# Key sums one level earlier, K turned one level later, the bonus product behind W: a reordering of the RWKV-7 chunk stage

## The chip, the cores and the metric

One core of a Trainium2 chip. The metric is the device time of one execution in microseconds (us). The kernel is written out instruction by instruction for five engines that run side by side: TensorE (PE, with its weight loads as PEld), VectorE (DVE), ScalarE (ACT), GpSimd (POOL) and SyncE (SP, which here only issues DMAs). Each engine takes its instructions strictly in the order in which they are written; engines meet only at semaphores.

## The reference, cut to what matters

One layer of a hybrid backbone over 2048 latent and 256 context tokens: norm, one wide input projection, four mixers in parallel, gates, an output projection. The change touches only one of the mixers, a two-way RWKV-7 recurrence over 4 heads of 64:

```
kk = to_heads(k * lp['rw_kk'])
kk = kk / jnp.maximum(jnp.sqrt(jnp.sum(kk * kk, axis=-1, keepdims=True)), 1e-12)
for d in range(2):
    w = -jax.nn.softplus(-(lp['rw_w0'][d] + jnp.tanh(w_lo) @ lp['rw_w2'][d])) - 0.5
    decay = to_heads(jnp.exp(-jnp.exp(w)))
    a = to_heads(jax.nn.sigmoid(lp['rw_a0'][d] + a_lo @ lp['rw_a2'][d]))
    kd = kh * (1.0 + (a - 1.0) * k_a)
    y, s_fin = wkv7_scan(rh, decay, kd, vh, -kk, kk * a, s0[d], reverse=(d == 1))
    bonus.append(jnp.sum(rh * kd * r_k, axis=-1, keepdims=True) * vh)
# one step of the scan
sa = jnp.einsum('bhvk,bhk->bhv', S, a_t)
S = S * w_t[:, :, None, :] + sa[..., :, None] * b_t[..., None, :] + v_t[..., :, None] * k_t[..., None, :]
```

The kernel computes the scan in chunks of 64 tokens. In each chunk the operands are scaled by the running decay ("hats": A from kk, R from r, K from kd, B from kk * a), a 64x64 triangular matrix is inverted by doubling, and what comes out are a map of the state (P), an addition to it (Q) and two terms of the output.

## The kernel before

`recurrence_local_stage` (from 1310 to 1788 us of the trace) works on 9 blocks of 256 tokens, each in two directions: 18 passes, d = 0 and d = 1 in turn, called `unit` on each engine. While a pass runs, the next one is prepared between its steps, so 17 passes hold a preparation: the 9 of d = 0 prepare d = 1 of the same block, 8 of d = 1 prepare d = 0 of the next block. That second preparation is the longer one: it also mixes the token rows and computes the inverse norm of kk.

TensorE's order in a pass, for the levels v = 1 to 5 of the inversion (`unit` in the tensor block): the product Gv (rows of the trace `rw_ps<-inv,m_b`), something beside it (`beside`), then Xv (`rw_ps<-inv_g,inv_t`) and Zv (`rw_ps<-inv_t,inv_g`), then something between (`between`). VectorE must mask Gv before Xv can start (`inv_g<-rw_ps`); ScalarE copies Xv and Zv to SBUF (`inv`, `inv_t`) before the next level's products can read them. At level 5 there is no X5.

- Beside level 3 stand a product of the preparation (`a_lora`, `rw_ps<-z_mixed,lora`) and the turning of K hat for the current pass (`rw_ps<-ident,k_hat`), which ScalarE copies out as `k_rows`. Between 3 and 4: `rw_ps<-head_centre,z_mixed` (V).
- Beside level 4 stand the key sums (`rw_ps<-heads,kk_sq`, in bank 4, where X4 is written too, so X4 waits until VectorE has read them into `kk_norm_sq`, "nx"). In a d = 1 pass VectorE then takes ten short dependent steps of Newton's method (`norms`, n0 to n2c) and spreads the result into rows (`kk_norm_rows`, "rx"). In a d = 0 pass the key sums are computed too, but nobody reads them.
- Between 4 and 5: `rw_ps<-ident,a_r_hat` (A). ScalarE copies it out as `w_in_rows` ("At."), and a second copy to the other half of that tile follows ("MV.").
- Beside level 5: `rw_ps<-v_rows,m_k`, and then the turning of the norm rows (`norm_columns`, `rw_ps<-ident,kk_norm_rows`, "rnT"), which is written to bank 7 and so waits for the copy At. Then Z5.
- Then the bonus product (`rw_ps<-kd_sum,heads`), W (`rw_ps<-w_in_rows,inv_t`), which waits for ScalarE's copy of Z5, and the first product of the next pass (`first_scores`, `rw_ps<-a_r_hat,b_hat`), which waits for VectorE's last hat; then GY (`rw_ps<-m_r,w_rows` and `rw_ps<-m_k,v_rows`).

ScalarE holds, besides the copies, the preparation's activations: `k_rate` (key rates, `key_rates`), and `exps`: `e_padded` (EI), `e_neg` (EN) and a tiny copy `chunk_decay` (tot). VectorE holds the scan of the logs (`decay`, `log_run`), `norms`, `rates` (`k_d`) and, at the end of the pass, `hats`.

Semaphores count results in a fixed order per engine (class `Turns`); the lists at the head of the stage (`prep_v`, `main_a`, `main_p` and others) name that order, and `after(engine, unit, result)` waits for one.

## Time and profile before

| | us |
|---|---|
| median of 3 runs | 2466.56 |
| lowest and highest | 2465.54, 2466.60 |
| the profiled execution's own time | 2462.29 |
| its span, first to last instruction | 2460.6 |
| TensorE busy, whole span | 2263.6 (92%) |
| VectorE busy | 1551.8 (63%) |
| ScalarE busy | 1009.5 (41%) |
| mean granted TensorE clock | 0.969 |

Busy time is what the profiler recorded for instructions of an engine; a matmul's end is modelled. A row of the timeline gives the start in us from the span's start, the duration, engine, line, operation, and what is written from what; in square brackets stands how long the engine was idle just before it and which instruction ended that. An f32 matmul is recorded as two, so 16 matmuls read x32. Neighbouring groups overlap in the rows by about 0.2 us because matmuls are pipelined; the distance from start to start is what a group costs.

### The profile page before, as it was taken

Reading aid. Unit: us, or ns where it says so; the run is one execution under the profiler, and the core shown is the slowest. Engines: PE = TensorE matmul, PEld = TensorE weight load, DVE = VectorE, ACT = ScalarE, POOL = GpSimd, SP = SyncE. Lnnn points to the kernel's source line nnn. Section 1 sums busy time; section 2 is a strip of 40 time slices with the busy share of each in tenths; the row PEclk is TensorE's granted clock in tenths of the full one; section 3 lists DMA queues with packets and bytes.
Section 4 is the critical chain, followed back from the end, with each engine's and each line's share of the span. In section 5 each row is a group of like instructions: output and inputs, shape, how many; then the busy total and the mean of one; then the engine's idle time right before and its main releaser. Section 6 shows DMA issues by size and latency. Waiting matters only on the chain. (4 is left out here: it accounts for less than half of the span.)

```text
span 2460.6 us, 66375 instructions
## 1 busy us (share of the span) xinstructions
PE 2263.6 (92%) x26630; PEld 1853.4 (75%) x26630; DVE 1551.8 (63%) x2611; ACT 1009.5 (41%) x1734; POOL 265.3 (11%) x335
## 2 busy tenths in 40 slices
PE   4999999999899999999947899999788799899998
PEld 2788878888688887888836777777657576688887
DVE  5756566666865456665635777777456676856754
ACT  5444234544532123445424555555333666411111
POOL 0000000000000000000031222222124663000000
PEclk7999999999999999999978999999978899999999
DMA  7344333333242333333330111110068523834542
GB/s 240 107 135 125 111 94 111 113 117 102 94 129 93 96 108 97 106 111 119 107 101 25 32 41 32 32 56 17 19 214 305 126 94 95 288 115 171 197 152 88
DMA packets 250306, 277.75 MB, mean 113 GB/s; under 512 B 30683, under 2 KB 174171, under 8 KB 247643
## 3 DMA queue, kind: packets, MB, share of 16 engines
q1 hardware_dynamic: 245306, 266.95, 33.9%
q10 hardware_dynamic: 4576, 8.40, 0.9%
q8 instruction: 70, 1.15, 0.2%
q0 software_dynamic: 320, 0.98, 0.2%
q14 instruction: 34, 0.27, 0.0%
HBM read 184.66 MB, written 91.62 MB: 112 GB/s over the span
## 5 line engine op out<-in xcount | busy, mean ns | idle before, releaser
L715 PE MATMUL proj_ps<-h_hi,w_hi 128*128 128x512 f32 x1656 | 649.5, 392 | 27.6 <-DVE h_lo L465 19.7
L716 PE MATMUL proj_ps<-h_lo,w_hi 128*128 128x512 f32 x1656 | 647.0, 391 | 0.0
L717 PE MATMUL proj_ps<-h_hi,w_lo 128*128 128x512 f32 x1656 | 646.4, 390 | 0.0
L318 ACT CAST w_hi<-w_raw 128x512 fp32r<-128x512 f32 x420 | 255.1, 621 | 694.0 <-PE proj_ps L717 353.2
L715 PEld LDWEIGHTS proj_ps<-h_hi,w_hi 128*128 128x128 f32 x1656 | 312.3, 189 | 98.2 <-issue 26.1
L717 PEld LDWEIGHTS proj_ps<-h_hi,w_lo 128*128 128x128 f32 x1656 | 312.2, 189 | 65.6
L716 PEld LDWEIGHTS proj_ps<-h_lo,w_hi 128*128 128x128 f32 x1656 | 312.4, 189 | 62.9
L482 DVE TENSOR_TENSOR w_lo<-w_raw,w_hi 128x512 fp32r<-128x512 f32 x420 | 283.2, 689 | 44.3 <-ACT w_hi L318 43.7
L498 DVE TENSOR_TENSOR z_slots<-proj_ps,x_rows 128x512 f32<-128x512 f32 x174 | 120.2, 691 | 169.9 <-PE proj_ps L717 167.9
L498 DVE TENSOR_TENSOR x_rows<-proj_ps,x_rows 128x512 f32<-128x512 f32 x116 | 80.1, 691 | 108.9 <-PE proj_ps L717 102.9
L1010 POOL MEMSET rpb_padded<- 60x127 f32 x1 | 0.2, 198 | 1261.3 <-POOLq L89 1261.3
L1211 DVE TENSOR_TENSOR inv_g<-rw_ps,level_masks 128x512 f32<-128x512 f32 x90 | 62.1, 690 | 97.2 <-PE rw_ps L1387 97.1
L2903 PE MATMUL late_ps<-late_lo,mw_hi 128*128 128x512 f32 x252 | 98.0, 389 | 0.0
L1334 ACT COPY inv<-rw_ps 128x512 f32<-128x512 f32 x72 | 42.0, 583 | 125.0 <-PE rw_ps L1387 125.0
L494 DVE COPY x_rows<-proj_ps 128x512 f32<-128x512 f32 x58 | 40.0, 690 | 73.6 <-PE proj_ps L717 73.5
L2492 DVE CUSTOM_DVE_ANT_0 scores<-na_ps,bias_windows 128x768 f32<-128x768 f32 x64 | 61.3, 957 | 34.4 <-issue 25.3
L2448 ACT ACTIVATE late_rows<-scores,softmax_stats 128x768 f32<-128x768 f32 x64 | 60.1, 940 | 52.3 <-DVE softmax_stats L2495 52.3
L2945 PE MATMUL late_ps<-wo_hi,y_hi 128*128 128x512 f32 x208 | 81.3, 391 | 0.0
L2947 PE MATMUL late_ps<-wo_hi,y_lo 128*128 128x512 f32 x208 | 81.0, 389 | 0.0
L2946 PE MATMUL late_ps<-wo_lo,y_hi 128*128 128x512 f32 x208 | 80.9, 389 | 0.0
L332 ACT ACTIVATE z_slots<-z_slots 128x512 f32<-128x512 f32 x128 | 70.6, 621 | 14.1 <-DVE z_slots L498 9.0
L2728 ACT ACTIVATE late_ps<-late_rows 128x1024 f32<-128x1024 f32 x15 | 15.4, 1030 | 125.8 <-DVE late_rows L2818 125.8
(380 smaller groups left out, 4101.4 us busy)
## 6 DMA issues: line engine op xcount, KB each, us to landing
w_raw<-in_w_in SPq DMA_DIRECT2D x240, 256.0 KB, 3.0
scratch_gatesT<-z_slots SPq DMA_DIRECT2D x128, 256.0 KB, 2.7
late_rows<-scratch_gatesT SPq DMA_DIRECT2D x64, 512.0 KB, 4.4
scratch_zT<-z_slots SPq DMA_DIRECT2D x108, 256.0 KB, 2.4
ada<-in_ada_w SPq DMA_DIRECT2D x4, 2048.0 KB, 15.2
late_rows<-scratch_zT SPq DMA_DIRECT2D x4, 2048.0 KB, 12.7
late_rows<-scratch_branchT SPq DMA_DIRECT2D x16, 512.0 KB, 5.3
late_rows<-in_x SPq DMA_DIRECT2D x16, 512.0 KB, 4.9
```

The costliest lines, as they stand in the source:

```text
L318: A.copy(wh[:, i, :, :], raw[:, q, :, :]).then_inc(w_hi, 1)
L332: A.activation(zs[:, q, :], zs[:, q, :], ACT.Sigmoid).then_inc(gated, 1)
L482: V.tensor_tensor(wl[:, i, :, :], raw[:, W_SOURCE[i], :, :], wh[:, i, :, :].bitcast(F32), ALU.subtract).then_inc(w_lo, 1)
L498: V.tensor_tensor(to, ps[:, BANK[n], :], part[:, {1: 0, 3: 0, 4: 2, 5: 0, 6: 1}[n], :], ALU.add).then_inc(ev, 1)
L715: T.matmul(out, wh[:, i, k, :], hi[:, o, k, :], start=(first and k == 0), stop=False, skip_group_check=not first)
L716: T.matmul(out, wh[:, i, k, :], lo[:, o, k, :], start=False, stop=False, skip_group_check=not first)
L717: last = T.matmul(out, wl[:, i, k, :], hi[:, o, k, :], start=False, stop=(k == 3), skip_group_check=not first)
L1211: done(V.tensor_tensor(eights(G[:]), ps[:, 2:4, 0:256].rearrange("p q (k t) -> p q k t", t=CH), mask, ALU.mult), f"G{v}.", *(("P0.", "Q0." ...
L2903: T.matmul(o, hi, b_lo[:, i % 2, k, :], start=False, stop=False)
L2945: T.matmul(o, y_hi[:, k, rows], wo_hi[:, k, cols], start=(k == 0), stop=False)
L2946: T.matmul(o, y_hi[:, k, rows], wo_lo[:, k, cols], start=False, stop=False)
L2947: last = T.matmul(o, y_lo[:, k, rows], wo_hi[:, k, cols], start=False, stop=(k == KT - 1))
```

## The change

It moves instructions of the stage; the arithmetic is the same. On TensorE the key sums go from beside level 4 to beside level 3, where they take the place of K's turning, which goes beside level 4; the wait for nx goes from X4 to X3, and the bonus product goes behind W. On ScalarE the key rates stay behind the third Z but now come ahead of the copy V; EI goes ahead of the copy of K's rows, and EN and tot go ahead of the copy At. On VectorE nx goes ahead of the scan and the ten Newton steps behind it, both to level 3; the spreading (rx) stays at level 4; one hat (R, or kk * a for d = 1) moves to an earlier place, and the last hat is now K, not B.

```
@@ beside(v), tensor block
                     if v == 3:
                         if more:
                             a_lora(u, -1)
+                            key_sums(u, -1)
+                    if v == 4:
                         main_a.after(pe, u, "Bt.")
                         go()
                         turned(Kh, "K.")
-                    if v == 4 and more:
-                        key_sums(u, -1)
@@ between(v)
                     if v == 4:
-                        main_a.after(pe, u, "V.")
+                        main_a.after(pe, u, "Kt.")
@@ unit, tensor block
-                    if v == 4 and more:
+                    if v == 3 and more:
                         prep_v.after(pe, u, "nx", -1)
...
-                if more:
-                    prep_v.after(pe, u, "bt", -1)
-                    go()
-                    prep_p.done(mm(ps[:, 6, :], J[:], flat(kds[:])), 0, "bonus")
                 main_a.after(pe, u, "Z5.")
...
                 done(last, "W.")
                 if more:
+                    prep_v.after(pe, u, "bt", -1)
+                    go()
+                    prep_p.done(mm(ps[:, 6, :], J[:], flat(kds[:])), 0, "bonus")
                     first_scores(u, -1)
@@ first_scores, tensor block
-                prep_v.after(pe, u, "B", back)
+                prep_v.after(pe, u, "K", back)
@@ unit, scalar block
                 factor(X[:], "X3.", 4)
                 factor(Z[:], "Z3.", 0)
-                rows(Kt, "Kt.", "K.")
+                if nxt:
+                    key_rates(*nxt)
                 if d == 0:
                     main_p.after(act, (n, d), "V.")
                     own(A.copy(flat(Vt[:]), ps[:, 6, :]), "V.")
                 if nxt:
-                    key_rates(*nxt)
+                    exp_up(*nxt)
+                rows(Kt, "Kt.", "K.")
                 factor(X[:], "X4.", 4)
                 factor(Z[:], "Z4.", 0)
+                if nxt:
+                    exp_down(*nxt)
                 main_p.after(act, (n, d), "A.")
                 own(A.copy(eights(WI[:, :, :, :, 0:CH]), ps[:, 6:8, 0:256].rearrange("p q (k t) -> p q k t", t=CH)), "At.")
-                if nxt:
-                    exps(*nxt)
@@ unit, vector block
                     if v == 3 and nxt:
+                        if d:
+                            norm_squares(nxt[0])
                         decay(*nxt)
+                        if d:
+                            norms(nxt[0])
+                        else:
+                            key_rate_hat(*nxt)
                     if v == 4 and nxt:
                         if d:
-                            norms(nxt[0])
+                            norm_rows(nxt[0])
                         rates(*nxt)
                         if d == 0:
                             bonus_rows(n)
+                        else:
+                            query_hat(*nxt)
@@ new helpers (exp_up is the first half of exps, exp_down its rest: EN and tot)
+            def norm_squares(n):
+                prep_p.after(dve, (n, 0), "ks")
+                prep_v.done(V.tensor_scalar(nx[:], ps[:, 4, 0:8], 1e-24, None, ALU.max), 0, "nx")
+            def key_rate_hat(n, d):
+                prep_a.after(dve, (n, d), "ta1")
+                prep_v.done(V.scalar_tensor_tensor(kka[:], aa[:], 1.0, kk[:], ALU.add, ALU.mult), d, f"kka{d}")
+            def query_hat(n, d):
+                prep_a.after(dve, (n, d), "EI")
+                if not (first_block(n) and d == 0):
+                    main_g.after(dve, (n, d), "R.", back=1)
+                prep_v.done(V.tensor_tensor(chunks(AR[:, 1, :, :]), chunks(zf[:, 0:2, :]), padded(d, 1 - d), ALU.mult), d, "R")
@@ hats: what is left, in the new order
+                if d:
+                    query_hat(n, d)
+                else:
                     prep_p.after(dve, (n, 0), "rnT")
                     done(V.tensor_tensor(kk[:], kkr[:], ps[:, 7, :].rearrange("p (m t) -> p m t", m=2), ALU.mult), "kk")
+                    prep_v.after(dve, (n, 0), "kk")
+                    key_rate_hat(n, d)
...
                 done(V.scalar_tensor_tensor(chunks(AR[:, 0, :, :]), chunks(kk[:]), -1.0, padded(d, d), ALU.mult, ALU.mult), "A")
+                prep_v.after(dve, (n, d), f"kka{d}")
+                prep_a.after(dve, (n, d), "EN")
+                done(V.scalar_tensor_tensor(Bh[:], kka[:], 0.5, EN[:], ALU.mult, ALU.mult), "B")
                 prep_v.after(dve, (n, d), "kd")
                 done(V.tensor_tensor(Kh[:], kd[:, d], EN[:], ALU.mult), "K")
-                prep_v.after(dve, (n, d), "kka")
-                done(V.scalar_tensor_tensor(Bh[:], kka[:], 0.5, EN[:], ALU.mult, ALU.mult), "B")
```

The result lists of the semaphores follow the new order; the preparation ahead of the first pass takes its steps in the new order too.

TensorE's queue in a pass, from the second preparation product beside level 3 to X3, before (`main_` and `prep_` semaphores belong to the current pass and to the preparation):

```order
L1387 MATMUL rw_ps<-z_mixed,lora 128x256 [waits prep_scalar]
L1387 MATMUL rw_ps<-z_mixed,lora 128x256
L1448 MATMUL rw_ps<-ident,k_hat 128x128 [waits main_scalar]
L1448 MATMUL rw_ps<-ident,k_hat 128x128 x3
L858 REGISTER_ALU
L1387 MATMUL rw_ps<-inv_g,inv_t 64x64 [waits main_scalar,main_vector]
```

and now (the line numbers are those of the changed kernel):

```order
L1416 MATMUL rw_ps<-z_mixed,lora 128x256 [waits prep_scalar]
L1416 MATMUL rw_ps<-z_mixed,lora 128x256
L1416 MATMUL rw_ps<-heads,kk_sq 128x2 [waits prep_vector]
L1416 MATMUL rw_ps<-heads,kk_sq 128x2 x3
L858 REGISTER_ALU
L858 REGISTER_ALU [waits main_scalar]
L1416 MATMUL rw_ps<-inv_g,inv_t 64x64 [waits prep_vector,main_vector]
```

K's turning has left this place, the key sums stand in it, and X3 behind them waits for `prep_vector` (nx) as well.

ScalarE's queue in a d = 1 pass from the third Z to the copies into `w_in_rows`, before:

```order
L1334 COPY inv_t<-rw_ps 128x512 [waits main_products]
L1338 COPY k_rows<-rw_ps 128x512 [waits main_products]
L1305 ACTIVATE k_rate<-a_tanh,one_less_half_ka,half_ka 128x256 [waits prep_scalar]
L1305 ACTIVATE k_rate<-a_tanh,one_less_half_ka,half_ka 128x256
L1334 COPY inv<-rw_ps 128x512 [waits main_products]
L1334 COPY inv_t<-rw_ps 128x512 [waits main_products]
L1367 COPY w_in_rows<-rw_ps 128x8x64 [waits main_products]
L1311 ACTIVATE e_padded<-log_run 128x8x64 [waits prep_vector]
L1312 ACTIVATE e_neg<-log_run 128x512
L1315 COPY chunk_decay<-e_padded 128x8 [waits prep_scalar]
L1371 COPY w_in_rows<-rw_ps 128x8x64 [waits main_products]
```

and now:

```order
L1361 COPY inv_t<-rw_ps 128x512 [waits main_products]
L1330 ACTIVATE k_rate<-a_tanh,one_less_half_ka,half_ka 128x256 [waits prep_scalar]
L1330 ACTIVATE k_rate<-a_tanh,one_less_half_ka,half_ka 128x256
L1334 ACTIVATE e_padded<-log_run 128x8x64 [waits prep_vector]
L1365 COPY k_rows<-rw_ps 128x512 [waits main_products]
L1361 COPY inv<-rw_ps 128x512 [waits main_products]
L1361 COPY inv_t<-rw_ps 128x512 [waits main_products]
L1338 ACTIVATE e_neg<-log_run 128x512
L1341 COPY chunk_decay<-e_padded 128x8 [waits prep_scalar]
L1398 COPY w_in_rows<-rw_ps 128x8x64 [waits main_products]
L1400 COPY w_in_rows<-rw_ps 128x8x64 [waits main_products]
```

Two instructions, `e_neg` and `chunk_decay`, now stand between the copy of Z4 and the first copy into `w_in_rows`; before, they stood behind it.

## Rows read from the trace of the kernel before

**Rows 1.** Busy time by stretch; columns as in the first row.
```profile
core 0: us, PE busy (x) PEld busy (x) DVE busy (x) ACT busy (x) POOL busy (x), PEclk, DMA share, GB/s
...
1310.00:1788.00 478.00, 422.83 (x15574) 362.83 (x15574) 327.54 (x633) 256.70 (x546) 103.49 (x95) 1.00 0.11 33
```

**Rows 2.** TensorE's waits, 1310 to 1788: us in total, times, longest.
```profile
PE rw_ps L1387 <- DVE b_hat L1152: 14.0, 17, 0.9
...
PE rw_ps L1387 <- DVE kk_norm_inv L1120: 3.5, 8, 0.4
```

**Rows 3.** TensorE timeline, d = 1 pass: start, us, ..., [idle before].
```profile
1505.75 0.66 PE L1448 MATMUL rw_ps<-ident,k_hat 128*128 128x128 f32 x4
1506.33 0.69 PE L1387 MATMUL rw_ps<-inv_g,inv_t 64*64 64x64 f32 x32
...
1508.51 0.69 PE L1387 MATMUL rw_ps<-inv,m_b 64*64 64x64 f32 x32
1509.14 1.05 PE L1387 MATMUL rw_ps<-heads,kk_sq 128*128 128x2 f32 x8
1510.63 0.69 PE L1387 MATMUL rw_ps<-inv_g,inv_t 64*64 64x64 f32 x32 [0.44 <-DVE kk_norm_inv L1120]
...
1513.21 0.66 PE L1426 MATMUL rw_ps<-ident,kk_norm_rows 128*128 128x128 f32 x4
1514.17 0.69 PE L1387 MATMUL rw_ps<-inv_t,inv_g 64*64 64x64 f32 x32 [0.30 <-issue]
1514.80 1.12 PE L1387 MATMUL rw_ps<-kd_sum,heads 128*128 128x512 f32 x2
1515.85 1.10 PE L1387 MATMUL rw_ps<-w_in_rows,inv_t 64*64 64x128 f32 x32
1517.82 1.10 PE L1387 MATMUL rw_ps<-a_r_hat,b_hat 64*64 64x128 f32 x32 [0.86 <-DVE b_hat L1152]
1518.71 0.44 PE L1387 MATMUL rw_ps<-m_r,w_rows 64*64 64x64 f32 x16
```

**Rows 4.** ScalarE timeline, the same pass.
```profile
1512.34 0.61 ACT L1367 COPY w_in_rows<-rw_ps 128x512 f32<-128x512 f32 x1
...
1513.35 0.65 ACT L1312 ACTIVATE e_neg<-log_run 128x512 f32<-128x512 f32 x1
...
1513.97 0.61 ACT L1371 COPY w_in_rows<-rw_ps 128x512 f32<-128x512 f32 x1
1514.92 0.59 ACT L1334 COPY inv_t<-rw_ps 128x512 f32<-128x512 f32 x1 [0.35 <-PE rw_ps L1387]
```

**Rows 5.** VectorE timeline, the same pass.
```profile
1505.94 1.22 DVE L1109 TENSOR_TENSOR_SCAN log_run<-scan_keep,log_w 128x512 f32<-128x512 f32 x1
1509.28 0.69 DVE L1211 TENSOR_TENSOR inv_g<-rw_ps,level_masks 128x512 f32<-128x512 f32 x1 [2.11 <-PE rw_ps L1387]
1510.23 0.17 DVE L1119 TENSOR_SCALAR kk_norm_sq<-rw_ps 128x8 f32<-128x8 f32 x1 [0.26 <-PE rw_ps L1387]
...
1512.44 0.43 DVE L1125 COPY kk_norm_rows<-kk_norm_inv 128x512 f32<-128x512 f32 x1
```

**Rows 6.** TensorE timeline, d = 0 pass.
```profile
1534.68 0.69 PE L1387 MATMUL rw_ps<-inv,m_b 64*64 64x64 f32 x32
1535.31 1.05 PE L1387 MATMUL rw_ps<-heads,kk_sq 128*128 128x2 f32 x8
1536.29 0.69 PE L1387 MATMUL rw_ps<-inv_g,inv_t 64*64 64x64 f32 x32
...
1539.46 0.69 PE L1387 MATMUL rw_ps<-inv_t,inv_g 64*64 64x64 f32 x32
...
1543.12 1.10 PE L1387 MATMUL rw_ps<-a_r_hat,b_hat 64*64 64x128 f32 x32 [0.87 <-DVE b_hat L1152]
```

**Rows 7.** VectorE timeline before the first pass.
```profile
1293.99 1.22 DVE L1109 TENSOR_TENSOR_SCAN log_run<-scan_keep,log_w 128x512 f32<-128x512 f32 x1
1297.51 0.17 DVE L1119 TENSOR_SCALAR kk_norm_sq<-rw_ps 128x8 f32<-128x8 f32 x1 [2.30 <-PE rw_ps L1387]
```

More of the change, by code:

```diff
@@ L918, in recurrence_local_stage @@
         U = 64
-        mixes, newton = [f"{j}" for j in (6, 2, 3, 0, 1, 4, 5)], ["nx", "n0"] + [f"n{i}{x}" for i in range(3) for x in "abc"] + ["rx"]
-        block_v = [f"mix{j}" for j in mixes] + ["ksq"] + newton + ["kk"]
+        mixes, newton = [f"{j}" for j in (6, 2, 3, 0, 1, 4, 5)], ["n0"] + [f"n{i}{x}" for i in range(3) for x in "abc"]
+        block_v = [f"mix{j}" for j in mixes] + ["ksq", "nx"] + newton + ["rx", "kk"]
         block_a = [f"scaled{j}" for j in mixes] + ["th", "kkr0", "kkr1", "rrk0", "rrk1"]
-        prep_v = Turns(ctx, nc, "prep_vector", [f"mix{j}" for j in mixes] + ["ksq", "lw", "L", "Lx", "inc"] + newton
-                       + ["kd", "kds", "bt", "kk", "R", "kka", "A", "K", "B", "bonus"], U,
-                       leaves_out=(("Lx", "inc", "kds", "bt", "bonus"), block_v))
+        prep_v = Turns(ctx, nc, "prep_vector", [f"mix{j}" for j in mixes] + ["ksq", "nx", "lw", "L", "Lx", "inc"] + newton + ["kka1", "rx", "kd"]
+                       + ["kds", "bt", "R", "kk", "kka0", "A", "B", "K", "bonus"], U,
+                       leaves_out=(("Lx", "inc", "kka1", "kds", "bt", "bonus"), block_v + ["kka0"]))
         prep_a = Turns(ctx, nc, "prep_scalar", [f"scaled{j}" for j in mixes]
@@ L1117, in norms @@
                 i32 = mybir.dt.int32
-                prep_p.after(dve, (n, 0), "ks")
-                own(V.tensor_scalar(nx[:], ps[:, 4, 0:8], 1e-24, None, ALU.max), "nx")
                 own(V.tensor_scalar(ny[:].bitcast(i32), nx[:].bitcast(i32), -0.5, 1597463007.0, ALU.mult, ALU.add), "n0")
@@ L1179, in prologue @@
                 key_squares(0)
+                norm_squares(0)
                 decay(0, 0)
                 norms(0)
+                norm_rows(0)
                 rates(0, 0)
+                query_hat(0, 0)
                 hats(0, 0)
@@ L1305, in key_rates, with exp_up, exp_down @@
                     prep_a.done(A.activation(uu[:, m, :], aa[:, m, :], ACT.Identity, scale=hka[:, m:m + 1], bias=oka[:, m:m + 1]), d, f"u{m}")
-            def exps(n, d):
+            def exp_up(n, d):
+                prep_v.after(act, (n, d), "inc" if d else "L")
+                prep_a.done(A.activation(padded(d, 1 - d), chunks((inc if d else L)[:]), ACT.Exp, scale=0.5 * DECAY), d, "EI")
+            def exp_down(n, d):
                 own = lambda ins, name: prep_a.done(ins, d, name)
-                prep_v.after(act, (n, d), "inc" if d else "L")
-                run = chunks((inc if d else L)[:])
-                own(A.activation(padded(d, 1 - d), run, ACT.Exp, scale=0.5 * DECAY), "EI")
                 own(A.activation(EN[:], (inc if d else L)[:], ACT.Exp, scale=-0.5 * DECAY), "EN")
@@ L1325, in prologue @@
                 key_rates(0, 0)
-                exps(0, 0)
+                exp_up(0, 0)
+                exp_down(0, 0)
                 act.sem_inc(main_a.sem, main_a.each)
```

15 lines of the change are left out of this document (5 added, 10 removed).

## Prediction

> **What bounds the kernel now.** I read the busy time by stretch first, then TensorE's waits in the stage that the change touches, then the timelines of three engines over two neighbouring passes. In the stage from 1310 to 1788 us TensorE is busy 422.8 of 478 us at the full granted clock, 1.00 [rows 1]: it is the bound, and time can only come from its waits or from work that it would no longer do. The change takes no work from it. The waits are few and regular: 14.0 us for VectorE's last hat ahead of the next pass's first product, 17 times, and 3.5 us, 8 times, ahead of X4 in d = 1 passes, where the view names the instruction behind nx [rows 2]. The question is how far each product starts later or earlier than before, and I follow that through one d = 1 and one d = 0 pass. Everything after the next pass's first product hangs on it by the same waits as before, so a shift there is the shift of the whole pass.
>
> **d = 1 pass (8 times).** Key sums at level 3. They start where K's turning stood, at 1505.75. Where they stand now, nx starts 1.09 us after them (1509.14 to 1510.23) and X4, waiting for it, 1.49 after them (1509.14 to 1510.63) [rows 3, 5]. X3 therefore starts at 1505.75 + 1.49 = 1507.24 and not at 1506.33: +0.91. G4, behind it, comes at about 1509.40.
>
> The Newton steps ahead of G4's mask. VectorE now waits with the scan until nx is read: nx at 1506.84, then the short op on log_w and the scan, which starts about 0.6 later and takes 1.22 [rows 5], so it ends near 1508.7. The ten steps follow; from nx to rx were 2.21 us, 0.20 of it nx itself, so they last 2.0 and end at 1510.7 [rows 5]. The mask of G4 stands behind them. It started 0.77 after G4 (1508.51 to 1509.28) [rows 3, 5] and would be wanted at 1510.17, so it is 0.5 late. In the d = 0 pass X4 starts 1.61 after G4 (1534.68 to 1536.29) [rows 6]: 0.77 to the mask, 0.69 for it, 0.15 to X4. So X4 follows the mask's start by 0.85 and comes at 1511.55 against 1510.63: +0.92. K's turning, now beside G4, takes 0.58 (1505.75 to 1506.33) and lies under this. Bounds: if the Newton steps were free, X4 would be 1.61 after G4, as in the d = 0 pass [rows 6], and the shift +0.4; if each small op cost some more for the wait between them, +1.1. I take 0.92, from the rows of the same ops.
>
> EN and tot ahead of the copy At. EN starts at 1513.35 and the copy behind tot at 1513.97, so the pair costs ScalarE 0.62 [rows 4]. At follows X4 by 1.71 (1510.63 to 1512.34), now by 2.33. Is anyone waiting? The norm rows' turning starts at 1513.21; At ended at 1512.34 + 0.61 = 1512.95, 0.26 before [rows 3, 4]. The product ahead of it is only 16 short matmuls, so I read the turning as waiting for At, and the 0.62 goes through in full. If it were TensorE's own queue that held it, up to 0.6 less: this is the lower bound. The turning takes 0.58, so Z5 starts at 1511.55 + 2.33 + 0.87 + 0.58 = 1515.33 against 1514.17: +1.16. (The old Z5 stood 0.96 after the turning, since G5's mask was late; that wait goes.)
>
> The bonus behind W. ScalarE's copy of Z5 starts at 1514.92 and takes 0.59; 0.15 later W can start, that is 1.49 after Z5. Before, the bonus product (1514.80 to 1515.85, 1.05) held W until 1.68 after Z5: 0.2 gained there [rows 3, 4]. W gives way to the next group after some 0.9, as the equal-shaped first product does (1517.82 to 1518.71). So W at 1516.82, bonus at 1517.71, first product at 1518.76 at the earliest. VectorE: the turned norms end at 1514.75 + 0.66 = 1515.41; then kk, kk * a (0.12 more, as it waits for kk), A, B, K at 0.60 each, and 0.68 + 0.15 to the first product: 1518.80. Both against 1517.82: +1.0. The old idle 0.86 ahead of the first product is gone, but the bonus fills it and the pass is not shorter.
>
> **d = 0 pass (9 times).** Nobody waits for nx here, so only the key sums' length against K's counts: 1.05 busy with a last matmul of 0.25, so about 0.93 from start to start, at most 0.98 (1535.31 to 1536.29) [rows 6], less 0.58: +0.35 at X3. At level 4 X4 is 1.61 after G4 because of the mask, and K's turning fits under that: +0.35. EN and tot: +0.62. Z5 is at +0.97. From Z5 to the first product are now 1.49 + 0.9 + 1.05 = 3.44 against 3.66 (1539.46 to 1543.12) [rows 6]: +0.75. The hat kk * a of d = 1 lies in VectorE's idle time ahead of G4, and the last hat is ready before TensorE asks.
>
> **Ahead of the first pass.** The scan ended before nx (1293.99 + 1.22 against 1297.51) and now stands behind it [rows 7]; some 1.8 us of it and the log come ahead of the Newton steps, of which one hat fewer behind rnT and a stall behind the Newton steps give back most. I take +0.5, between 0.3 and 1.2. The last pass has no preparation: no change.
>
> **A rule against one of these terms.** The row: eight passes of the key sums, with only 2 columns each, take 1.05 us [rows 3]. The Trainium skill, "TensorE: Matmul & The Clock Gate", section "Back-to-back issue gap", gives for 1 to 64 columns an issue floor of about 25 ns; by that the key sums would be some 0.2 us, shorter than K's turning, and X3 in a d = 0 pass would come 0.4 earlier and not 0.35 later. The same page's section "LDWEIGHTS" lets a load of 128 columns take 107 ns, which is near what the row shows. By the first rule the nine d = 0 passes alone would be 9 x 0.7 = 6.3 us cheaper and the sum some 9 us instead of 15. The measured row decides, and it speaks for the longer figure.
>
> **Sum.** 8 x 1.0 + 9 x 0.75 + 0.5 = 8.0 + 6.75 + 0.5 = 15.3 us. The profiled execution took 2462.29 us and would take 2477.6. It lies 4.27 below the median of 2466.56; by the median the forecast is 2481.8, rounded 2482.
>
> **Rivals.**
> 1. ScalarE's EN and tot are covered: the norm rows' turning did not wait for At. For it: the product ahead of it starts only some 0.6 before. Against: the steady 0.26 behind At's end. Then the d = 0 pass shifts by 0.13 and the d = 1 pass by 0.4: 8 x 0.4 + 9 x 0.13 + 0.5 = 4.9, 2471.5 us, on the edge of no change. 10%.
> 2. Faster: TensorE's waits on VectorE are the whole price. The mechanism is at the end of the pass and at X3: key sums cost there no more than K's turning did, nx is ready before X3 is due, and the earlier hats let the bonus run in the idle time before the first product. It decides if nx comes within 0.6 us of the key sums' start and EN is covered. Then a d = 0 pass gains the 0.2 at W, a d = 1 pass that, the 0.44 ahead of X4 and the 0.38 of the late G5 mask: 9 x 0.2 + 8 x 1.0 = 10, 2456.6 us. For it are the 17.5 us of waits in [rows 2]; against it the 1.09 us that nx took. 6%.
> 3. Much slower: TensorE's clock. It is 1.00 in the stage with idle times below 0.9 us [rows 1, 3]. The new wait ahead of X3 is 0.44 us, and ahead of X4 it is 0.8 or so. Should these waits bring it to its lower level (1.2 instead of 2.4 GHz), products take twice as long there; for 2 us of products in each d = 1 pass that is 8 x 2 = 16 on top, 2498 us. The rows show no fall in 478 us after idle times nearly as long. The Trainium skill, "TensorE: Matmul & The Clock Gate", section "Part 1: The HAM clock gate", says that activity releases the throttle and idleness brings it back. That the clock stayed at 1.00 through the waits of before does not contradict it. This rival has 4%.
>
> **Numbers.** The forecast's own case has 80%. Within it the terms are uncertain by 0.4 us per pass at most, mostly downwards (Newton steps, the key sums' length), so 2476 to 2486. Taking in part of rival 1, the range is 2473 to 2487. A measurement of this kernel tells 0.2%, 5 us, from no change. Faster 7%, same 9%, slower 84%.
>
> **What would show it.** In the changed kernel's timeline: in a d = 1 pass 1.5 us from key sums to X3; G4's mask right behind the last Newton step and later than 0.77 after G4; X4 2.1 to 2.2 after G4; in both passes At 2.3 after X4 and the norm rows' turning 0.87 behind At's start; bonus between W and the first product with no idle time between the three. Passes about 1.0 and 0.75 us longer. The forecast is wrong if the turning of the norm rows starts less than 3 us after X4 in the d = 0 pass, if X3 follows the key sums by less than 1.2 us in the d = 1 pass, or if the granted clock is not 1.00.

## The result and the profile after

The changed kernel takes 2481.47 us (median of 6 runs, 2473.41 to 2484.22) against 2466.57 (6 runs, 2462.32 to 2467.01) for the kernel before, run beside it: ratio 1.0059, 95% interval 1.0045 to 1.0073: slower by 0.6%. The profiled execution took 2484.22 us, its span is 2482.5 against 2460.6. A pass is counted here from the start of its G1 (rows `rw_ps<-inv_first,m_b`), which is 4.6 us behind what is called its first product, to that of the next; passes are numbered 1 to 18, the odd ones are d = 0. Where the 21.9 us of span come from:

| part of the span | before | after | difference |
|---|---|---|---|
| to the first product of the stage | 1290.51 | 1294.02 | +3.5 |
| from there to the first pass | 19.90 | 22.73 | +2.8 |
| the 18 passes | 476.74 | 496.28 | +19.5 |
| behind the stage | 673.35 | 669.41 | -3.9 |

The change touches neither the first nor the last part, and the two nearly cancel. The passes in the loop last 25.26 to 25.30 (d = 0) and 26.81 to 26.83 (d = 1) before; after, 26.10 to 26.16 and 27.86 to 28.09, or 28.51 to 28.53 in four of the eight d = 1 passes. So a d = 0 pass is some 0.85 longer and an undisturbed d = 1 pass 1.18; four d = 1 passes have 0.52 on top. Passes 2 to 16 together are 17.4 us longer, the first 0.7. One stop of TensorE's queue that waits for nothing (3.87 us in before, in pass 17) stands in pass 18 in after, with 3.18 us. Outside this stop pass 17 is 0.8 longer and pass 18, which has no preparation, still 1.3.

The busy time by stretch in the changed kernel, with the columns of [rows 1]; the last two rows are neighbouring stretches within a d = 1 pass:

```profile
1290.00:1310.00 20.00, 6.97 (x20) 4.83 (x20) 5.92 (x18) 6.09 (x12) 3.48 (x14) 0.50 0.13 24
1310.00:1804.00 494.00, 429.68 (x15359) 369.20 (x15360) 331.85 (x635) 255.81 (x542) 93.90 (x95) 0.97 0.10 32
...
1570.70:1574.10 3.40, 3.07 (x72) 2.49 (x64) 1.31 (x3) 3.20 (x7) 0.40 (x1) 1.00 0.00 0
1574.20:1577.60 3.40, 3.08 (x69) 2.99 (x70) 3.00 (x11) 1.57 (x3) 0.00 (x0) 0.50 0.00 0
```

TensorE is busy 429.7 of 494 us: some 7 us more busy time than in [rows 1] (2.8 of it products that before lie ahead of 1310) and 9 us more idle. And the granted clock of the stage is 0.97, not 1.00: between 1574.2 and 1577.6 it is 0.50, the lower of its two levels (1.2 GHz), right behind a stretch at full speed. The waits of TensorE in the stage, us in total, times, longest, beside [rows 2]:

```profile
PE rw_ps L1416 <- ACT inv_t L1361: 13.5, 17, 0.8
...
PE rw_ps L1455 <- ACT w_in_rows L1398: 8.6, 16, 0.5
...
PE rw_ps L1416 <- DVE k_hat L1166: 3.4, 1, 3.4
PE rw_ps L1416 <- DVE kk_norm_sq L1117: 2.8, 8, 0.3
```

The 14.0 us for VectorE's last hat are gone; in their place stand 8.6 us in 16 waits for ScalarE's copy At, 2.8 for nx (3.5 before), and the waits for Z5's copy ahead of W (13.5, 17 times). The 3.4 us for `k_hat`, once, lie ahead of the first pass. TensorE's timeline: a d = 1 pass, beside [rows 3]; then key sums and X3 of a d = 1 pass at half clock; then a d = 0 pass, beside [rows 6]:

```profile
1518.96 1.05 PE L1416 MATMUL rw_ps<-heads,kk_sq 128*128 128x2 f32 x8
1520.37 0.69 PE L1416 MATMUL rw_ps<-inv_g,inv_t 64*64 64x64 f32 x32 [0.35 <-DVE kk_norm_sq L1117]
...
1522.55 0.69 PE L1416 MATMUL rw_ps<-inv,m_b 64*64 64x64 f32 x32
1523.17 0.66 PE L1477 MATMUL rw_ps<-ident,k_hat 128*128 128x128 f32 x4
1524.93 0.69 PE L1416 MATMUL rw_ps<-inv_g,inv_t 64*64 64x64 f32 x32 [1.11 <-issue]
...
1528.12 0.63 PE L1455 MATMUL rw_ps<-ident,kk_norm_rows 128*128 128x128 f32 x4 [0.54 <-ACT w_in_rows L1398]
...
1530.16 1.10 PE L1416 MATMUL rw_ps<-w_in_rows,inv_t 64*64 64x128 f32 x32 [0.80 <-ACT inv_t L1361]
1531.20 1.12 PE L1416 MATMUL rw_ps<-kd_sum,heads 128*128 128x512 f32 x2
1532.26 1.10 PE L1416 MATMUL rw_ps<-a_r_hat,b_hat 64*64 64x128 f32 x32
...
1573.12 1.05 PE L1416 MATMUL rw_ps<-heads,kk_sq 128*128 128x2 f32 x8
1574.52 1.13 PE L1416 MATMUL rw_ps<-inv_g,inv_t 64*64 64x64 f32 x32 [0.35 <-DVE kk_norm_sq L1117]
...
1605.72 0.69 PE L1416 MATMUL rw_ps<-inv_g,inv_t 64*64 64x64 f32 x32 [0.27 <-issue]
...
1608.90 0.63 PE L1455 MATMUL rw_ps<-ident,kk_norm_rows 128*128 128x128 f32 x4 [0.53 <-ACT w_in_rows L1398]
```

X3 starts 1.41 after the key sums (1518.96 to 1520.37). X4 is 2.38 behind G4 (1522.55 to 1524.93) where it was 2.12 [rows 3]; the view calls its wait of 1.11 "issue", and the next fence shows what it was. The turning of the norm rows waits 0.54 in d = 1 and 0.53 in d = 0, both times for At. Between W, bonus and first product there is no idle time, and W waits 0.80 for Z5's copy. VectorE, two rows ahead of the first pass and then the d = 1 pass, beside [rows 7] and [rows 5]:

```profile
1304.71 0.17 DVE L1126 SCALAR_TENSOR_TENSOR kk_norm_inv<-kk_norm_step,kk_norm_inv 128x8 f32<-128x8 f32 x1
1307.38 0.43 DVE L1129 COPY kk_norm_rows<-kk_norm_inv 128x512 f32<-128x512 f32 x1 [2.50 <-issue]
...
1520.05 0.17 DVE L1117 TENSOR_SCALAR kk_norm_sq<-rw_ps 128x8 f32<-128x8 f32 x1 [1.33 <-PE rw_ps L1416]
...
1521.94 0.17 DVE L1122 TENSOR_SCALAR kk_norm_inv<-kk_norm_sq 128x8 int32<-128x8 int32 x1
...
1523.85 0.17 DVE L1126 SCALAR_TENSOR_TENSOR kk_norm_inv<-kk_norm_step,kk_norm_inv 128x8 f32<-128x8 f32 x1
1524.14 0.69 DVE L1228 TENSOR_TENSOR inv_g<-rw_ps,level_masks 128x512 f32<-128x512 f32 x1
```

The last of the ten small steps starts at 1523.85 and G4's mask only at 1524.14, 1.59 after G4 (0.77 in [rows 3, 5]); X4 follows the mask's start by 0.79. ScalarE in the same pass, beside [rows 4]:

```profile
1526.65 0.64 ACT L1338 ACTIVATE e_neg<-log_run 128x512 f32<-128x512 f32 x1
1527.18 0.21 ACT L1341 COPY chunk_decay<-e_padded 128x8 f32 x1
1527.28 0.60 ACT L1398 COPY w_in_rows<-rw_ps 128x512 f32<-128x512 f32 x1
```

EN and tot take 0.63 (1526.65 to 1527.28), and At starts right behind them; TensorE's turning at 1528.12 follows At's end (1527.88) by 0.24, as it did before (0.26).

### The profile page after: what moved, and what is told of

Its sections match the earlier page's. It is cut to its first block and busy times, and to the rows that moved or that the text cites. A ratio compares the mean times of both kernels' runs of the same rounds, so it can differ in the third digit from the quotient of the medians.

```text
span 2482.5 us, 66412 instructions
## 1 busy us (share of the span) xinstructions
PE 2271.8 (92%) x26630; PEld 1859.9 (75%) x26630; DVE 1554.5 (63%) x2611; ACT 1011.1 (41%) x1734; POOL 254.1 (10%) x335
## 3 DMA queue, kind: packets, MB, share of 16 engines
q8 instruction: 70, 1.15, 0.2%
## 5 line engine op out<-in xcount | busy, mean ns | idle before, releaser
L1416 PE MATMUL rw_ps<-inv_g,inv_t 64*64 64x64 f32 x2304 | 61.8, 232 | 12.1 <-issue 9.3
## 6 DMA issues: line engine op xcount, KB each, us to landing
ada<-in_ada_w SPq DMA_DIRECT2D x4, 2048.0 KB, 15.3
```

## The experiments

Each starts from the changed kernel ("after") or the kernel before, and its passes are read undisturbed unless said otherwise. Offsets are from a pass's start.

**EN and tot behind At** (from after).

```
@@ unit, scalar block
-                if nxt:
-                    exp_down(*nxt)
                 main_p.after(act, (n, d), "A.")
                 own(A.copy(eights(WI[:, :, :, :, 0:CH]), ...), "At.")
+                if nxt:
+                    exp_down(*nxt)
```

> The changed kernel with one edit: ScalarE's EN and tot go back behind the copy At; all else as changed. My theory (EN and tot sit on the path from Z4 through At to the norm rows' turning, Z5, W): the turning starts 0.62 us earlier behind X4, each of the 17 passes with a preparation is 0.6 us shorter (d = 0 passes 26.13 to about 25.5, d = 1 passes 28.0 to about 27.5), 17 x 0.6 = 10 us in all, about 2471 us. Rival (At is not waited for, TensorE's own queue holds the turning): passes within 0.1 us of 26.13 and 28.0, total unchanged at 2481.

2475.0 us (7 runs, 2468.92 to 2481.7) against 2464.9: 1.0039, interval 1.0020 to 1.0058. Passes 25.59 and 27.41, so 0.51 to 0.57 and 0.59 shorter than after. TensorE in a d = 0 pass:

```profile
1548.21 0.69 PE L1416 MATMUL rw_ps<-inv_g,inv_t 64*64 64x64 f32 x32 [0.28 <-issue]
...
1550.78 0.65 PE L1455 MATMUL rw_ps<-ident,kk_norm_rows 128*128 128x128 f32 x4
1551.37 0.69 PE L1416 MATMUL rw_ps<-inv_t,inv_g 64*64 64x64 f32 x32
```

The turning starts 2.57 after X4 (1548.21 to 1550.78), with no idle time before it; in after it was 3.18 (1605.72 to 1608.90). EN and tot had gone through nearly in full: rival 1 is out. The medians differ by 6.5 us, less than the passes promise (9 x 0.54 + 8 x 0.59 = 9.6 us): eight of the 16 passes behind the first hold a stretch at half clock here, and a d = 0 pass with one takes 27.05 to 27.11, 1.5 more. That is taken up below.

**The Newton steps back behind G4's mask** (from after; nx stays ahead of X3).

```
@@ unit, vector block
                         decay(*nxt)
-                        if d:
-                            norms(nxt[0])
-                        else:
+                        if d == 0:
                             key_rate_hat(*nxt)
                     if v == 4 and nxt:
                         if d:
+                            norms(nxt[0])
                             norm_rows(nxt[0])
```

> The changed kernel with one edit: the ten Newton steps go back behind VectorE's mask of G4 (nx stays at level 3, ahead of the scan). My theory (the steps hold G4's mask in d = 1 passes): G4 to X4 shrinks from 2.39 to 1.6 us in d = 1 passes; the steps then run behind the mask at level 4 and may hold the norm rows' turning or G5's mask, so the pass gains between 0.3 and 0.8 us of its 28.0; d = 0 passes stay at 26.13. Rival (the steps fit in idle time and X4 waits for something else, for instance for the copy of Z3 or K's turning): G4 to X4 stays above 2.2 us and the d = 1 pass within 0.1 us of 28.0.

2483.54 us (one run). X4 comes at 15.24 instead of 16.07, but the d = 1 pass is 28.14, no shorter than after's 28.00: the 0.3 to 0.8 that were expected did not come. VectorE and TensorE of one such pass:

```profile
1524.59 0.68 DVE L1133 TENSOR_TENSOR k_d<-k_rate,z_mixed 128x512 f32<-128x512 f32 x1
...
1525.19 1.10 DVE L1148 TENSOR_TENSOR a_r_hat<-z_mixed,e_padded 128x512 f32<-128x512 f32 x1
...
1526.21 0.68 DVE L1228 TENSOR_TENSOR inv_g<-rw_ps,level_masks 128x512 f32<-128x512 f32 x1
...
1526.99 0.69 PE L1415 MATMUL rw_ps<-inv_t,inv_g 64*64 64x64 f32 x32 [0.86 <-issue]
```

rx, k_d and R (1.10 long here) now follow the steps, so that G5's mask starts only at 1526.21, and Z5 waits 0.86 for it. The 0.83 is given back there: Z5 is at 19.89 against 19.81. The ten steps delay one mask or the other; their place in the change is no loss by itself.

**Only the bonus product behind W** (from before).

```
@@ unit, tensor block
-                if more:
-                    prep_v.after(pe, u, "bt", -1)
-                    go()
-                    prep_p.done(mm(ps[:, 6, :], J[:], flat(kds[:])), 0, "bonus")
                 main_a.after(pe, u, "Z5.")
...
                 if more:
+                    prep_v.after(pe, u, "bt", -1)
+                    go()
+                    prep_p.done(mm(ps[:, 6, :], J[:], flat(kds[:])), 0, "bonus")
                     first_scores(u, -1)
```

> The kernel before with one edit: the bonus product behind W instead of ahead of it. My theory (the idle time ahead of the next pass's first product belongs to VectorE's last hat and the bonus merely fills it): W starts 1.49 instead of 1.68 us behind Z5, the bonus fills the idle time, and the first product still waits for the last hat; passes within 0.1 us of 25.28 and 26.82. Rival (the waits of 0.87 us ahead of the first product are recovered): passes shorter by 0.5 to 0.87 us, 8 to 15 us in all. Second rival: the bonus is longer than the gap and adds 0.2 us.

2464.41 us (one run); passes 25.25 and 26.77 against 25.28 and 26.82.

TensorE in a d = 1 pass:

```profile
1516.73 1.10 PE L1387 MATMUL rw_ps<-w_in_rows,inv_t 64*64 64x128 f32 x32 [0.79 <-ACT inv_t L1334]
1517.77 1.12 PE L1387 MATMUL rw_ps<-kd_sum,heads 128*128 128x512 f32 x2
1518.89 1.10 PE L1387 MATMUL rw_ps<-a_r_hat,b_hat 64*64 64x128 f32 x32
```

The bonus fills the time in which TensorE waited for the last hat, W comes 0.2 earlier, and the next pass starts as before. Rival 2 took this for a gain; it is none, since the hat comes no earlier. **The same with B ahead of K** as well (VectorE's last two hats exchanged, the first product waiting for K):

> The kernel before with the bonus product behind W and with B ahead of K among VectorE's hats, the first product still waiting for B only. My theory (with the bonus behind W, the first product waits for VectorE's last hat; one hat fewer ahead of it makes TensorE's queue the bound): the first product 3.45 us behind Z5 instead of 3.66; passes 25.06 and 26.6 instead of 25.26 and 26.77, 3.4 us less in all. Rival (VectorE's later steps, bonus and mask, then come late by the same): passes unchanged.

2462.73 us (11 runs), 0.9993, interval 0.9983 to 1.0003; passes 25.19 and 26.71. A tenth of a microsecond per pass, within no change.

**Only the exchange of key sums and K's turning** (from before): tensor block as in the change at levels 3 and 4, nx ahead of the scan, K's copy behind the key rates; Newton steps, EN and tot, hats and bonus where they were.

> The kernel before with one edit: key sums beside level 3, K's turning beside level 4, the wait for nx at X3 and nx ahead of the scan; Newton steps, exponentials, hats and bonus as before. My theory: d = 0 passes longer by 0.35 (key sums 0.93 against K 0.58), d = 1 passes by 0.4 (0.91 more at X3 for the wait on nx, 0.5 less at X4). Rival (the key sums with 2 columns each cost no more than K's turning, and nx is early): d = 0 passes unchanged, d = 1 passes shorter by up to 0.44.

2480.24 us (one run). X3 is at 10.44 (d = 0) and 11.50 (d = 1), exactly as in after, X4 at 14.17 and 15.24; the passes are 25.59 and 27.05, so +0.33 and +0.23. That is 9 x 0.33 + 8 x 0.23 = 4.8 us. Seven of passes 2 to 16 took some 1.5 us more each (27.11 to 27.17 instead of 25.6, 28.40 to 28.59 instead of 27.06), 10.5 us. The two together are what this run lies above 2464.9, the median of before beside it. A stretch of the first of the seven:

```profile
1378.70:1382.10 3.40, 3.40 (x72) 3.28 (x72) 1.71 (x3) 1.17 (x2) 0.51 (x1) 0.50 0.00 0
```

TensorE is busy all the time, at half clock.

**The same with TensorE given more to do there**: K's turning is issued a second time, right behind the key sums, into bank 7, where nobody reads it.

```
@@ beside(3), tensor block of the exchange alone
                             key_sums(u, -1)
+                            main_a.after(pe, u, "Bt.")
+                            go()
+                            ... (four transposes of Kh into ps[:, 7])
```

> The kernel with the swap alone, with K's turning issued once more beside level 3, behind the key sums (its result is thrown away; the one at level 4 counts). Theory on the clock (it falls because TensorE does little around the key sums and X3's wait): no stretch at half clock in passes 2 to 16; d = 0 passes at 26.2 (0.58 more than 25.6), d = 1 passes at 27.1 to 27.2, no pass at 28.5. Rival (the falls come with the phase of the passes or with something else): as many stretches at half clock as with the swap alone, where 8 of 15 passes had one.

2473.88 us (one run), 6 less, although every pass has a turning more (26.1 and 27.18). Two of passes 2 to 16 hold a half-clock stretch instead of seven. (The expectation says 8 of 15 for the exchange alone; it was 7.) The added turning also makes every pass longer, so this run does not tell what TensorE does at that place from where in the pass the stretches fall.

**Only EI, EN and tot ahead of At** (from before): `exps` stands ahead of the copy At and is otherwise whole.

> The kernel before with all three, EI, EN and tot, ahead of the copy At, nothing else. My theory: At and the norm rows' turning come 1.15 us later behind X4 in both kinds of pass. In d = 0 passes R starts 0.5 earlier and the gap ahead of the first product takes most of the rest, so the pass is longer by about 0.1 only; in d = 1 passes the turned norms come late for kk and the pass is longer by 1.1 (27.9). Rival (ScalarE's exponentials are covered): turning unchanged, passes within 0.1 of 25.28 and 26.82.

2478.68 us (one run), passes 25.92 and 27.80: +0.64 and +0.98. In d = 0 that is far above what was expected. The missing step, in a d = 0 pass:

```profile
1604.68 0.63 PE L1426 MATMUL rw_ps<-ident,kk_norm_rows 128*128 128x128 f32 x4 [1.05 <-ACT w_in_rows L1369]
...
1606.92 1.10 PE L1387 MATMUL rw_ps<-w_in_rows,inv_t 64*64 64x128 f32 x32
1607.85 1.05 PE L1387 MATMUL rw_ps<-a_r_hat,b_hat 64*64 64x128 f32 x32
1609.31 0.46 PE L1387 MATMUL rw_ps<-m_r,w_rows 64*64 64x64 f32 x16 [0.41 <-ACT w_rows L1375]
```

The turning waits 1.05 for At, and W comes 1.09 later in the pass. The first product does not: it stands 20.70 us into the pass (20.66 before), since its old wait for the hat took the delay up. But GY behind it needs ScalarE's copy of W, which is as late as W is; it waits 0.41 for it and comes 0.60 later than before. I had followed the delay only to the first product.

**Key sums in bank 7** (from EN and tot behind At): the key sums are written to bank 7, not to X4's and X3's bank 4, so X3 does not wait for nx; the wait moves to K's turning. VectorE does the scan first, then nx and the Newton steps.

```
-                prep_v.done(V.tensor_scalar(nx[:], ps[:, 4, 0:8], ...), 0, "nx")
+                prep_v.own(dve, (n, 0), V.tensor_scalar(nx[:], ps[:, 7, 0:8], ...), "nx")
@@ beside(v), tensor block
                         if more:
                             a_lora(u, -1)
+                        main_a.after(pe, u, "Bt.")
+                        if more:
                             key_sums(u, -1)
                     if v == 4:
-                        main_a.after(pe, u, "Bt.")
+                        if more:
+                            prep_v.after(pe, u, "nx", -1)
                         go()
                         turned(Kh, "K.")
@@ unit, tensor block
-                    if v == 3 and more:
-                        prep_v.after(pe, u, "nx", -1)
```

> The changed kernel with EN and tot behind the copy At, and the key sums of level 3 written to bank 7 (free there) instead of bank 4, so that nx is waited for by K's turning and not by X3; nx and the Newton steps stand behind the scan. My theory (X3's wait for nx and the late scan are what level 3 costs): X3 comes 0.93 us behind the key sums in both kinds of pass, G4's mask is no longer late in d = 1 passes; undisturbed d = 0 passes 25.4, d = 1 passes 26.1 us (27.41 with the wait), about 2461 us if the granted clock stays at 1.00. Rival (the clock falls because the key sums themselves leave the array little to do, not because of the wait): stretches at half clock stay, 10 to 12 us into passes, each worth up to 1.5 us, and the time is 2465 to 2475.

2462.75 us (12 runs, 2457.53 to 2469.99) against 2463.73 (23 runs): 0.9999, interval 0.9990 to 1.0009. Passes 25.63 and 26.22. A d = 1 pass:

```profile
1612.21 1.05 PE L1415 MATMUL rw_ps<-heads,kk_sq 128*128 128x2 f32 x8
1613.19 0.69 PE L1415 MATMUL rw_ps<-inv_g,inv_t 64*64 64x64 f32 x32
...
1615.37 0.69 PE L1415 MATMUL rw_ps<-inv,m_b 64*64 64x64 f32 x32
...
1616.98 0.69 PE L1415 MATMUL rw_ps<-inv_g,inv_t 64*64 64x64 f32 x32 [0.33 <-DVE inv_g L1228]
```

X3 follows the key sums by 0.98, and the d = 1 pass is 1.19 shorter than with bank 4 (27.41). So what hung on nx was the whole rest of the price in d = 1, and more: 0.43 at X3, and with it the late mask (X4 is 1.61 after G4 again). The run does not tell the bank's part from that of the scan's place. Over the stage it is 9 x 0.35 - 8 x 0.60 = -1.7 us against before, and two stretches at half clock (27.13, 27.12) give back more than that: no change.

**A version that should beat both** (from the last one): V is computed in two halves, one between levels 3 and 4, one beside level 4; two rounds of Newton's steps ahead of G4's mask, the third behind it; kk * a for d = 1 back among the last hats, behind R; EI behind At in a d = 0 pass; ScalarE copies K's rows ahead of V; and the first product waits for B, the hat before the last.

```
@@ between(3) and beside(4), tensor block
-                        (V, 8 matmuls, between 3 and 4)
+                        values(0)
...
                         turned(Kh, "K.")
+                        done(values(1), "V.")
@@ unit, vector block
-                            norms(nxt[0])
+                            norms(nxt[0], range(2))
...
+                            norms(nxt[0], range(2, 3))
                             norm_rows(nxt[0])
```

> On the kernel with the key sums in bank 7 and EN behind At, in the loop of one pass: the product V parted in two halves, one between the third and the fourth level as before, one beside level 4 behind K's turning, where TensorE waits for G4's mask anyway; Newton steps parted around that mask; kk * a of d = 1 back among the last hats; for d = 0 EI stays behind At. Theory (TensorE's queue outside the fixed waits is the price, and level 4 has 1.0 us from G4 to X4 of which K's turning fills 0.6): 0.4 us less a pass than with the bank alone, d = 0 passes 25.2, d = 1 passes 25.8, a block 51.0 against 52.1 of before, 8 to 9 us less than before in all, ratio 0.9965. Rival (ScalarE's copies of K and V now come so late that its copy of X4 waits, or the clock falls behind the key sums as before): passes 25.6 and 26.2 or with stretches at half clock of 1.5 us each, ratio 0.999 to 1.002.

2451.34 us (6 runs, 2446.1 to 2454.01) against 2465.82 (11 runs): 0.9937, interval 0.9922 to 0.9953. It beats both kernels. Passes 25.19 and 25.84 as forecast (9 x 0.09 + 8 x 0.98 = 8.7 us), but for two d = 1 passes of 27.34 and 27.33 with a half-clock stretch; with these, passes 2 to 16 give 5.5 us. The profiled executions differ by 11.3 (span 2449.3): 1.1 more lie between the stage's first product and the first pass (18.81 instead of 19.90), 0.9 in the first pass, and 3.8 net in the last two passes and outside the stage. The medians differ by 14.5; the other 3.2 I cannot place. Around level 4:

```profile
1581.28 0.71 PE L1418 MATMUL rw_ps<-head_centre,z_mixed 128*128 128x128 f32 x4
1581.92 0.69 PE L1418 MATMUL rw_ps<-inv,m_b 64*64 64x64 f32 x32
1582.55 0.66 PE L1479 MATMUL rw_ps<-ident,k_hat 128*128 128x128 f32 x4
1583.04 0.61 PE L1418 MATMUL rw_ps<-head_centre,z_mixed 128*128 128x128 f32 x4
1583.58 0.69 PE L1418 MATMUL rw_ps<-inv_g,inv_t 64*64 64x64 f32 x32
```

X4 starts 1.66 after G4 with no idle time before it: half of V fills the fixed delay that G4's mask makes.

**No unread products**: key sums and norm rows in d = 0 and V and bonus in d = 1, whose results nobody reads, are not computed. For this TensorE's loop body holds two passes. First in before's order with bonus behind W and B ahead of K:

> The kernel with B ahead of K and the bonus behind W, its order of levels as before, and TensorE's loop written over two passes instead of one, so that it leaves out the products that nobody reads: key sums and norm rows in d = 0 passes, V and the bonus in d = 1 passes. Theory (what counts is TensorE's queue between fixed waits, so only products outside the idle times pay): d = 0 passes 25.1 (only the norm rows' turning was outside, by 0.07), d = 1 passes 25.6 (V 0.69 ahead of G4, the bonus up to VectorE's last hat), 12 to 13 us in all, 2451 us. Rival (a loop body of twice the length costs instruction fetches each time round, or the clock falls with TensorE idler): passes no shorter than 25.19 and 26.71 on average.

2565.16 us (5 runs), 1.0399, interval 1.0384 to 1.0414. Then from the key sums in bank 7, with Newton's steps parted:

> The same without the unread products, on the order of the changed kernel with its three costs mended: EN and tot behind At, key sums at level 3 written to bank 7 so that X3 does not wait for nx, and the Newton steps parted around G4's mask (two iterations ahead, one behind); kk * a of d = 1 back among the last hats, the first product waits for B. Theory: with the unread key sums gone, d = 0 passes have only one preparation product at level 3 and K's turning at level 4 is covered: 24.6 us; d = 1 passes 24.9 to 25.3. That is 2.3 us a block less than 52.1, some 20 us in all, 2443 us, and less than the same without the unread products in the order of before. Rival (VectorE takes over as the bound at levels 3 and 4, or the granted clock falls behind the now thinner level 3): blocks of 50.7 us or more, no better than the order of before.

2556.97 us (5 runs), 1.0376, interval 1.0361 to 1.0392. Less work, 4% slower. What is left in both is the length of the loop body. **Only that** (from before, every product kept):

```
-            with nc.Fori(E, 2 * NBLK * E, E, ...) as u:
-                unit(u, True)
+            with nc.Fori(E, (2 * NBLK - 1) * E, 2 * E, ...) as u:
+                unit(u, True)
+                unit(u, True, 1)
+            unit((2 * NBLK - 1) * E, True)
             unit(2 * NBLK * E, False)
```

> The kernel before with TensorE's loop written over two passes instead of one, nothing left out and nothing moved. Theory (the 4% of the two kernels without the unread products come from the length of the loop body: TensorE's instructions are fetched anew in each round): passes in the loop 4 to 10 us longer than before, groups of matmuls broken by idle times that end in no semaphore, over 150 packets in the instruction queue against 70, some 2560 us. Rival (leaving products out starves the clock, or a semaphore comes late): passes as before, 25.28 and 26.82, 2465 us.

2589.94 us (one run) against 2465.82. (Next to this, the kernel above that leaves the unread products out of the same loop, 2565.16, is 25 us faster: leaving them out seems to pay, and the loop takes back more.) Its timeline, and the row of its instruction queue (packets, MB):

```profile
1431.70 0.53 PE L1388 MATMUL rw_ps<-inv,m_b 64*64 64x64 f32 x18
1433.99 0.40 PE L1388 MATMUL rw_ps<-inv,m_b 64*64 64x64 f32 x12 [1.76 <-issue]
...
1443.37 0.62 PE L1388 MATMUL rw_ps<-b_hat,a_r_hat 64*64 64x64 f32 x26 [1.24 <-issue]
...
q8 instruction: 183, 3.00, 0.5%
```

A group of equal matmuls that depend on nothing new is broken in the middle (18, then 12 of 32) by 1.76 us of idle time. From 1343 to 1850 us TensorE's waits called "issue" come to 91.2 us in 56 (longest 2.8), against 6.2 us in 24 (longest 0.3) in passes 2 to 16 of before. The instruction queue moved 3.00 MB where the changed kernel and the one before move 1.15. The passes take 29.3 to 30.0 and 33 to 39 us. The cause is therefore the body's length; that it is the fetching of instructions is what the queue's count suggests.

## Why the prediction came out right, and where its terms were not

- **Key sums at level 3.** X3 +0.40 in d = 0 (said +0.35) and +0.81 in d = 1 (said +0.91, 1.49 behind the key sums; it is 1.41). Shown by the exchange alone, which has the same X3. The eight passes of the key sums take 0.98 from start to start where nothing waits (key sums in bank 7), 0.12 each. By that, of the two sections of the Trainium skill, "TensorE: Matmul & The Clock Gate", "LDWEIGHTS" fits (by its formula 107 ns for 128 columns, an estimate). The 25 ns of "Back-to-back issue gap" do not apply: the section gives them for an isolated matmul and says itself that at small sizes this leaves out the weight load, which the prediction passed over.
- **Newton steps ahead of G4's mask.** Said: mask 0.5 late, X4 +0.92. Measured: mask 0.82 late, X4 +1.08, at the upper bound given. The ten small steps and the scan took what the rows said; nx came to the hundredth as said; the ten steps ended 0.1 later, the mask started 0.12 behind their end, and G4 came 0.07 earlier. That moving them back would gain nothing I had not asked.
- **EN and tot ahead of At.** Said +0.62 with the turning 0.87 behind At's start. Measured 0.63, 0.84, and 0.51 to 0.59 of a pass. Shown by taking it out.
- **Bonus behind W.** No gain, as said. But W gives way after 1.04, not 0.9: the term of the sum that was mis-sized. W to bonus is 1530.16 to 1531.20. I had taken the 0.9 from the first product, behind which GY stands. It depends on what follows: where the first product stands right behind W, it starts 0.93 after it (EI, EN and tot ahead of At); the bonus starts 1.04 after W in the changed kernel and in the one with only the bonus moved. With the later mask it makes the first product +1.2 and +0.85 (said +1.0 and +0.75).
- **Ahead of the first pass.** Said +0.5, between 0.3 and 1.2; measured +2.8, outside the bounds. The order that the term is about costs +0.8, inside them: in the exchange alone, which takes nx ahead of the scan here too, this part lasts 20.67 us, with K's turning issued twice 20.68, against 19.90. What the changed kernel has on top is a stop: VectorE stands idle for 2.50 us between the last Newton step and rx, waiting for nothing that the trace shows, where the gap was 0.86 before. The stop is no accident of one execution: it stands at the same place with 2.52 and 2.50 in the two kernels with EN and tot or the Newton steps moved back, and with 2.74 one instruction earlier in the one with the key sums in bank 7; the exchange alone has none there, and the last version (18.81) only 0.83. What brings it is not shown. TensorE's clock is also still at 0.50 when the first pass begins (until about 1321.6); before, the pass began at 1.00. The first pass is nevertheless only 0.73 longer, since one stop of 1.71 us in it is gone.
- **The clock, rival 3.** It was given 4%, with 2 us in each d = 1 pass, 16 us in all. It came in small: four stretches of 3.4 us at 0.50, each beginning 11.16 us into a d = 1 pass, that is where the key sums end and X3's wait begins, each for +0.52: 2.1 us. The forecast said that a granted clock other than 1.00 would show it wrong, and in this point it was. Every kernel with the key sums at level 3 and the short loop body has two to eight of passes 2 to 17 with such stretches, all beginning 10.4 to 11.7 us into the pass, about where the key sums end, but for two in the kernel with the Newton steps moved back (at 20.8 and 21.1); in before and its variants with key sums at level 4 and the short loop body, passes 2 to 16 have none. The rival had taken the new waits for the cause. They are not needed: both stretches with the key sums in bank 7, and four of the seven in the exchange alone, stand in d = 0 passes, where X3 follows the key sums without idle time. With one turning more behind the key sums there were two instead of seven. The place is shown; that the key sums' small products bring the fall is suggested by it and not proved, since the seven and the two are single executions and the passes' lengths differ as well. The Trainium skill, the same page, "Part 1: The HAM clock gate", lets idleness bring the throttle back; the idle time of 0.35 us ahead of X3 is no longer than others at which the clock stayed at 1.00 (1.11 ahead of X4).
- **The last pass.** Said: no change. Outside its stop it is 1.3 us longer. It holds two stretches at 0.50, beginning some 4.6 and 14.9 us into it; in before it holds one, up to 3 us into it. That this is the reason is not shown.
- **The sum.** Said 15.3; the medians give 14.9 (interval 11.1 to 18.0). The profiled executions give more in what the change touches, 2.8 + 19.5 = 22.3. Against 15.3 that is 7.0 more, of which the passes' terms explain 2.2, the stretch ahead of them 2.3, the clock 2.1, and the last pass with its shorter stop 0.6. The profiled execution of after is the slowest of its six runs and that of before lies 4.3 below its median, so what of the 22.3 the other executions do not have stays open. The granted clock of the whole execution is the lowest of the six in the profiled one (0.963) and the highest, 0.967, in the fastest (2473.41) and one other (2479.54): the number of stretches may differ between executions, but only one was traced. So the forecast of 2482 is right in what it said of the passes, each wait at its place and most sizes within 0.2 us; the stop ahead of the first pass, the clock and the last pass it did not have, and that the medians show no more than the sum, to the half microsecond, is luck.
- **A reading.** The prediction calls TensorE's waits few, and names 14.0 and 3.5 us. The same view also has 18.9 us of "issue" in 33 waits and 11.5 us for ScalarE's copies of X in 28. The sum does not rest on them.

## What to carry to other kernels

A moved instruction is priced at the next thing that waits on its engine, and then at the one behind that: EN and tot cost 0.5 to 0.6 us of their 0.63 because the copy behind them was already the latest, and the ten Newton steps in one piece cost the same on either side of a mask. Look for fixed delays (here G, mask, X: about 1 us) and fill them to their length, no more; where a product waits only for a PSUM bank to be read, write to another bank first. Before unrolling a loop body to save work, measure the longer body alone.

## What the runs showed of the hardware

- A loop body of TensorE twice as long: 124 us more over 18 passes, and 3.00 MB of instructions for 1.15. The engine stops in the middle of a group, for 0.6 to 2.8 us, with no wait that the trace shows.
- TensorE's clock goes to 0.50 for 3.4 us in the middle of a loop that runs otherwise at 1.00, with TensorE busy 3.07 of the 3.40 us ahead of it, and with or without an idle time at the place. It costs 0.5 us in after and 1.5 in two of its variants, depending on what lies in the stretch, and it hits a different number of passes in kernels that differ little (none to eight). A gain of a few microseconds can drown in it.
- Idle times of 2.5 to 3.9 us that wait for nothing stand near the ends of the loop, and their place moves with the code: TensorE's 3.87 us in the last prepared pass before, 3.18 in the last pass after; VectorE's 2.50 to 2.52 ahead of rx in after and two of its variants, 2.74 one instruction earlier in a third, none in before.
